# Mixture-of-experts stage of a decoder trunk: sixteen groups of 64 slots in plain fp32 in place of four groups of 128 slots in split fp32r

## What is computed

```python
def route_gates(xt, router_w, router_b):
    scores = jax.nn.sigmoid((xt @ router_w).astype(jnp.float32))
    sel = scores + router_b.astype(jnp.float32)
    # best of 4 groups by the sum of its two best experts, then its two best experts
    ...
    return jnp.sum(jax.nn.one_hot(idx, N_EXPERTS, dtype=jnp.float32) * w[..., None], axis=1)

def grouped_moe(x, router_w, router_b, w_gate, w_up, w_down):
    gates = route_gates(xt, router_w, router_b).astype(x.dtype)
    for e in range(N_EXPERTS):
        h = jax.nn.silu(xt @ w_gate[e]) * (xt @ w_up[e])
        out = out + gates[:, e:e + 1] * (h @ w_down[e])
```

## Time and profile before

| | |
|---|---|
| median of 3 runs | 905.53 us (905.52 to 907.23) |
| the profiled execution, its own time | 907.88 us |
| its span, first to last instruction | 906.1 us |
| PE matmuls busy | 88% of the span |
| DVE / ACT busy | 70% / 51% |
| loaded from memory | 174 MB, 193 GB/s over the span |
| mean granted clock of PE | 0.944 of 2.4 GHz |

### The profile page before, as it was taken

One profiled execution on the slowest core, in us unless ns is written; L12 is line 12 of the kernel. 1 busy time (PEld: TensorE's weight loads), 2 busy tenths in 40 slices (PEclk: granted clock), 3 DMA queues, 4 the chain that ended last, 5 costly groups with the idle time before them and its releaser, 6 DMA issues.

```text
span 906.1 us, 13457 instructions
## 1 busy us (share of the span) xinstructions
PE 794.1 (88%) x5124; PEld 715.8 (79%) x5124; DVE 634.4 (70%) x941; ACT 463.7 (51%) x684; POOL 46.2 (5%) x88
## 2 busy tenths in 40 slices
PE   4998899999957999999679889999998599999993
PEld 4987777888847898999469678777976499989992
DVE  4756864745485997889658487566355769979985
ACT  3445343455452776767333553344445347757761
POOL 3300000100050000000010000001000000000000
PEclk9999999999977999999969999999999599999997
DMA  9952035753254798799544221467423229968931
GB/s 288 348 184 94 24 116 188 230 187 140 81 188 142 293 360 323 258 350 311 180 139 141 94 93 47 146 206 253 146 87 140 93 97 383 350 239 324 345 121 48
DMA packets 62531, 176.15 MB, mean 194 GB/s; under 512 B 3856, under 2 KB 37056, under 8 KB 53248
## 3 DMA queue, kind: packets, MB, share of 16 engines
q1 hardware_dynamic: 57856, 162.80, 51.2%
q0 software_dynamic: 4032, 12.24, 4.4%
q10 hardware_dynamic: 576, 0.20, 0.1%
HBM read 174.18 MB, written 1.05 MB: 193 GB/s over the span
## 4 chain that ended last, share of the span: by engine, by line
PE 73%; DVE 14%; DVEq 4%; issue 4%; ACT 3%; DMA 1%; POOL 0%; ACTq 0%; POOLq 0%; SPq 0%
PE ring L1408 16%; PE ring L1410 15%; PE ring L1409 15%; PE quad L1408 5%; PE quad L1409 5%; PE quad L1410 5%; DVE w_lo L837 3%; PE ring L1672 2%; PE ring L1651 2%; PE quad L1766 2%; DVE x_lo L856 1%; ACT w_hi L560 1%; DMA raw<-in_w_in 1%; PE ring L1547 1%; PE ring L1721 1%
## 5 line engine op out<-in xcount | busy, mean ns | idle before, releaser
L837 DVE TENSOR_TENSOR w_lo<-raw,w_hi 128x1024 fp32r<-128x1024 f32 (+1 forms) x244 | 283.9, 1206 | 107.9 <-ACT w_hi L560 104.4
L560 ACT CAST w_hi<-raw 128x1024 fp32r<-128x1024 f32 (+1 forms) x244 | 240.4, 1038 | 114.4 <-PE quad L1410 83.7
L1408 PE MATMUL ring<-x_hi,w_hi 128*128 128x256 f32 x480 | 143.8, 300 | 19.7 <-DVE x_lo L856 9.1
L1409 PE MATMUL ring<-x_lo,w_hi 128*128 128x256 f32 x480 | 140.9, 293 | 0.0
L1410 PE MATMUL ring<-x_hi,w_lo 128*128 128x256 f32 x480 | 140.7, 293 | 0.0
L1408 PEld LDWEIGHTS ring<-x_hi,w_hi 128*128 128x128 f32 x480 | 97.4, 203 | 24.9 <-issue 11.0
L1409 PEld LDWEIGHTS ring<-x_lo,w_hi 128*128 128x128 f32 x480 | 97.4, 203 | 0.5 <-issue 0.5
L1410 PEld LDWEIGHTS ring<-x_hi,w_lo 128*128 128x128 f32 x480 | 97.3, 203 | 0.0
L1408 PE MATMUL ring<-w_hi,x_hi 128*128 128x256 f32 x288 | 82.6, 287 | 2.8 <-DVE x_lo L1292 2.8
L1410 PE MATMUL ring<-w_hi,x_lo 128*128 128x256 f32 x288 | 82.2, 285 | 0.0
L1409 PE MATMUL ring<-w_lo,x_hi 128*128 128x256 f32 x288 | 82.1, 285 | 0.0
(11 more groups left out here) (271 smaller groups left out, 1508.1 us busy)
## 6 DMA issues: line engine op xcount, KB each, us to landing
raw<-in_moe_w_gate SPq DMA_DIRECT2D x32, 1024.0 KB, 4.9
raw<-in_moe_w_up SPq DMA_DIRECT2D x32, 1024.0 KB, 5.0
raw<-in_moe_w_down SPq DMA_DIRECT2D x32, 1024.0 KB, 5.1
raw<-in_w_in SPq DMA_DIRECT2D x14, 1024.0 KB, 8.5
raw<-in_xattn_wk SPq DMA_DIRECT2D x8, 1024.0 KB, 6.9
raw<-in_w_out SPq DMA_DIRECT2D x8, 1024.0 KB, 5.0
raw<-in_xattn_wv SPq DMA_DIRECT2D x8, 1024.0 KB, 4.9
raw<-in_xattn_wq SPq DMA_DIRECT2D x8, 1024.0 KB, 5.7
```

The costliest lines, as they stand in the source:

```text
L560: nc.scalar.copy(unit_slot(u, 0, n)[:, s], raw[:, u % RAW_SLOTS, s]).then_inc(hi_done, 1)
L837: last = nc.vector.tensor_tensor(unit_slot(u, 1, n)[:, s], raw[:, u % RAW_SLOTS, s], unit_slot(u, 0, n)[:, s].bitcast(F32), ALU.subtract)
L1408: mm(out, a_hi, b_hi, start=first, stop=False)
L1409: mm(out, a_hi, b_lo, start=False, stop=False)
```

## The change

In the branch for tokens that fit, nothing of the expert weights is split any more. The raw ring has ten buffers for the experts (six raw ones, and the four places of `w_hi` and `w_lo`, seen as plain fp32), and PE multiplies straight from them in plain fp32. The order of loads is gate and up of a pair of experts, then the downs of the pair before.

Slots belong to an expert and no longer to a group of four: 64 slots each, 1,024 in all; the branch is taken if no expert has over 64 tokens. A token appears in the slots of both its experts. The gather runs in four quarters of 256 slots, and its result is only copied (half by ACT, half by DVE), no longer split. An even expert uses rows 0 to 63 of the PSUM banks, an odd one rows 64 to 127; a pair's hidden tiles are transposed together, copied by ACT, and its outputs, one expert in each half of the rows, are split and scattered with 8 matmuls for each pair. The general branch is written out without loops and reads the raw weights too.

```diff
+def expert_units(n):
+    order = []
+    for j in range(n // 2):
+        order += [(what, e) for e in (2 * j, 2 * j + 1) for what in "gu"]
+        if j:
+            order += [("d", 2 * j - 2), ("d", 2 * j - 1)]
+    return order + [("d", n - 2), ("d", n - 1)]
...
+    RING = RAW_SLOTS + 2 * SPLIT_SLOTS
+    SLOT = [u % RAW_SLOTS for u in range(U_MOE)]
+    SLOT += [m % RING for m in range(3 * E - 2)] + [RING - 2, RING - 1]
...
+        def of_pair(e):
+            return slice(EXPERT_SLOTS * (e % 2), EXPERT_SLOTS * (e % 2) + EXPERT_SLOTS)
...
-                for k in range(3):
-                    hi(U_MOE + k, l, NORMAL)
                 norm_stats(1, l)
...
-                lo(U_MOE + 1, l, NORMAL)
                 for t in range(T):
                     dve.wait_ge(xn_hi_done, l * T + t + 1)
...
-                for g in range(N_GROUPS):
+                for q in range(E // PER_GROUP):
                     for t in range(T):
-                        nc.vector.tensor_scalar(to_slot(t)[:, g * P:(g + 1) * P], slots[:], place[:, t, g:g + 1],
-                                                grv[:, t, g:g + 1], ALU.is_equal, ALU.mult)
...
+                        nc.vector.tensor_tensor(to_slot(t)[:, 256 * q:256 * q + 256].rearrange("p (e s) -> p e s", e=4),
+                                                view(slots[:], [[0, PER_GROUP], [1, EXPERT_SLOTS]]),
+                                                view(mine, [[1, PER_GROUP], [0, EXPERT_SLOTS]]), ALU.is_equal)
+                    dve.drain().then_inc(slots_ready, 1)
...
+                    def project_slots(e):
+                        if e >= 2:
+                            pe.wait_ge(h_ready, l * E + (e - 1))
+                            pe.wait_ge(turned_moved, l * PAIRS + e // 2)
+                        rows, q = of_pair(e), e // PER_GROUP
+                        s = slice(EXPERT_SLOTS * (e % PER_GROUP), EXPERT_SLOTS * (e % PER_GROUP) + EXPERT_SLOTS)
+                        for i, u in enumerate((gate_unit(e), up_unit(e))):
+                            pe.wait_ge(raw_full[SLOT[u]], landed(u, l))
+                            w = slot_view(u).rearrange("p (c n) -> p c n", c=DC)
+                            for c in range(DC):
+                                r = mm(ring[rows, i, 0:FF], slots_of(q)[:, c, s], w[:, c, :], start=c == 0,
+                                       stop=c == DC - 1)
+                            r.then_inc(unit_used, 1)
...
+                    def down(j):
+                        pe.wait_ge(turned_moved, l * PAIRS + (j + 1))
+                        if 0 < j < PAIRS - 1:
+                            pe.wait_ge(out_split, l * PAIRS + j)
+                        for e in (2 * j, 2 * j + 1):
+                            rows, u = of_pair(e), down_unit(e)
+                            pe.wait_ge(raw_full[SLOT[u]], landed(u, l))
+                            w = slot_view(u).rearrange("p (c n) -> p c n", c=2)
+                            for a in range(2):
+                                for c in range(2):
+                                    r = mm(out_bank(j, a)[rows, :], h_t[:, j % 2, c * P:(c + 1) * P][:, rows],
+                                           w[:, c, 512 * a:512 * a + 512], start=c == 0, stop=c == 1)
...
-                    for k in range(E):
...
+                    gather(0)
+                    pe.wait_ge(quad_free, l * (3 * T) + 2 * T)
+                    gather(1)
+                    gathered_rows(0)
...
+                    gates_of_slots()
+                    project_slots(0)
+                    gathered_rows(1)
+                    gather(2)
+                    project_slots(1)
+                    gathered_rows(2)
+                    to_token_turns()
+                    turn(0)
+                    project_slots(2)
+                    project_slots(3)
+                    pe.wait_ge(to_token_moved, l + 1)
+                    gather(3)
+                    turn(1)
+                    down(0)
+                    gathered_rows(3)
+                    for j in range(2, PAIRS):
+                        project_slots(2 * j)
+                        project_slots(2 * j + 1)
+                        scatter(j - 2)
+                        turn(j)
+                        down(j - 1)
+                    down(PAIRS - 1)
+                    scatter(PAIRS - 2)
+                    scatter(PAIRS - 1).then_inc(moe_done, 1)
```

More of the change, by code:

```diff
@@ L439, in _ @@
                     load(U_O + i, l, src, (2, D))
[L440 to L449, removed]
+                for m, (what, e) in enumerate(MOE):
+                    expert(l, e, what, U_MOE + m)
             for t in range(T):
@@ L762, in _ @@
                     act.sem_inc(act_emptied, 8)
[L764 to L772, removed]
@@ L788, in _ @@
                     last.then_inc(to_token_moved, 1)
[L789 to L798, removed]
@@ L1217, in _ @@
                 dve.wait_ge(act_emptied, emptied("rt1", l))
-                score, sel, rank, weight, grp = (rt[:, i] for i in range(1, 6))
+                score, sel, rank, weight, grp, member = (rt[:, i] for i in range(1, 7))
                 nc.vector.tensor_scalar(score, score, 1.0, None, ALU.add)
@@ L1339, in _ @@
-                    turned_low(E - 1)
-                    out_low(N_GROUPS - 1)
+                    nc.vector.tensor_scalar(slot_gates[:], ring[:, 3, 0:E], 0.5, None, ALU.mult)
+                    dve.drain()
+                    hidden(0)
+                    gather_move(2)
+                    hidden(1)
+                    for j in range(1, PAIRS):
+                        hidden(2 * j)
+                        hidden(2 * j + 1)
+                        if j == 1:
+                            gather_move(3)
+                        out_low(j - 1)
@@ L1735, in turn, with gates_of_slots @@
-                    def turn(k):
-                        pe.wait_ge(dve_emptied, l * DVE_LAYER + (DVE_AHEAD + 2 * (k + 1)))
+                    def gates_of_slots():
+                        for j in range(PAIRS):
+                            for t in range(T):
+                                r = mm(ring[:, 3, 2 * j:2 * j + 2], to_slot(t)[:, j * P:(j + 1) * P].bitcast(F32),
+                                       gates[:, t, 2 * j:2 * j + 2], start=t == 0, stop=t == T - 1)
+                        r.then_inc(slot_gated, 1)
@@ L1859, in _ @@
-                    step(2, 0, 0, first=True)
-                    step(3, 0, 0)
-                    with pe.Fori(1, STEPS) as i:
-                        step(2, i * 6, i * 2)
-                        step(3, i * 6, i * 2)
-                    moe_down(0, down_unit(E - 2), 0, E - 2)
-                    moe_down(1, down_unit(E - 1), 0, E - 1, last=True)
-                    pe.sem_inc(gathered, 8)
+                    for e in range(E):
+                        if e >= 2:
+                            pe.wait_ge(h_ready, l * E + (e - 1))
+                        moe_in(2 * (e % 2), gate_unit(e))
+                        moe_in(2 * (e % 2) + 1, up_unit(e))
+                        if e % 2 and e >= 3:
+                            moe_down(e - 3)
+                            moe_down(e - 2)
```

493 lines of the change are left out of this document (231 added, 262 removed).

## The result

The median of four runs is **941.2 us** (937.9 to 944.2) against 905.6 us before: ratio 1.0387, 95% interval 1.0350 to 1.0425. Slower, as forecast, by 35.5 us where the sum said 47.8. The profiled execution took 941.9 us, with a span of 940.1.

A forecast was written before the change was run, and what follows sets the result against it. TensorE was taken to set the pace; a stage of 182.7 + 7.3 = 190.0 us against 166.1 added 47.8 us over two layers, giving 953 us on the median's scale, with 920 to 980 us for 8 in 10.

The forecast's parts named there:

- The step on which it hung: Expert matmuls: halves meet for 3 matmuls of 32, so a 64-wide one costs 0.216 us like a 128-wide one.
- Gate, up and down: Expert stage, per layer: gate and up 110.6 less 5.2 us, down 55.0 less 10.3 and 7.0; together 143 us.
- Bank 0 behind ScalarE's copies: Expert 2's gate waits until ScalarE has copied four slot matrices and then the tile itself: 2.9 us with semaphores.
- The pair waits: Each later pair waits on its last hidden tile, mostly covered by a scatter: 0.3 x 7 = 2.0 us.
- Going between 64 and 128 wide: TensorE in the expert stage: each switch of matmul width waits 0.1 us, x 26 = 2.6 us.
- A fetch behind the written-out general branch: Jumping past the general branch may cost a code fetch: bounds 0 and 3 us a layer, taken as 0.
- Gather, slot gates and matrices, transposed tiles and scatter: Rest of TensorE's stage work, 39.6 us: gather 17.8, gates 3.4, slot matrices 1.7, hidden tiles 1.7, scatter 15.0.
- What would be seen: New profile: gate/up 0.216 us apart, downs 0.43, gapless PE, DVE and ScalarE below 30%, DMA near 300 GB/s, stage 190 us.
- rival 4: Clock falls while half of the array works; gate, up and down would double: above 1,200 us, chance 0.02.
- Rival 1: Array halves run fully beside each other and loads decide: stage 128 us, -38 a layer, 830 us; chance 0.11.
- Rival 2: Reach about twice as long, seven matmuls meet and not three: 21 us less a layer, 912 us; chance 0.08.
- Rival 3: Waits between pairs don't hide (hidden tile, transpose, ScalarE's copy, down): 1.5 us x 16 pairs, 977 us; chance 0.04.

The follow-up runs named there:

- call by call: Changed kernel with a pair's gate, up and down calls alternating between its two experts, one call each in turn, loads reordered to match: 842.5 us, ratio 0.9291.

## Why the prediction was right, point by point

**The step on which it hung** was that 64 wide costs as much as 128 wide unless the halves alternate within some 7 instructions. It held, with 4 matmuls and their loads in place of 3, and the experiments show it from both sides: the same arithmetic in another order takes 842.5 us. The rule quoted from the Trainium skill, "TensorE: Matmul & The Clock Gate", "The mechanism" of Part 3, that matmuls go strictly first in, first out, is contradicted by the windows around 348.93 us. The 2x of column tiling that the Trainium skill's "TensorEngine Tiling (Array Packing)", "When to Use Tiling", gives for 64 columns is real (64 matmuls in 6.91 us), but only in an order of issue that it does not ask for.

**Terms of the first layer's stage**, predicted 190.0 us, measured 185.9 (from the first gather to VectorE's start at 466.52 us):
- Gate, up and down: 143.1 predicted, 140.4 measured (9.37 + 7.05 + 14.88, six pairs of 16.70, 8.90). 4.0 of it is half clock that I had not seen coming (2.3 at expert 0, 1.7 at expert 2). Without it 136.4, so 6.7 us too much in the sum. The halves meet for 4 matmuls, not 3. For the downs, which also meet once more between the last two pairs, that is 9 x 4 x 0.43 = 15.5 us against 10.3. Gate and up meet seven times and not the eight of the sum, since a gather lies between experts 0 and 1: 7 x 4 x 0.216 = 6.0 against 5.2. The last three downs cover 1.4 us of the next gates in six pairs, 8.5 against 7.0. Together 7.5 us; some 0.8 of it goes back because the first matmul of a run takes longer (32 in 7.05 us, not 6.91).
- Waits: 7.3 predicted, 3.7 measured. Bank 0 behind ScalarE's copies: 2.9 predicted, 2.25 measured. The pair waits (2.0) did not come: in the steady pair each piece starts where the last ends, to 0.02 us. Going between 64 and 128 wide (2.6) costs no wait either, but it lengthens the pieces: behind 64-wide matmuls the scatter's 8 take 2.06 us where the kernel before's took 1.87, and the first of a gather 0.32 where the next take 0.12. Ten such places make 1.9 us, counted below. The type changes there too, from plain fp32 to fp32r in most of them, so what part is due to the width is not shown.
- A fetch behind the written-out general branch: bounds 0 to 3, I took 0. After the first layer's stage VectorE starts 1.42 us late with nothing in the profile to wait for, and 3.7 us late call by call (beyond my bound of 3), both times in the first layer only:
```profile
462.10 3.00 PE quad L1795 x12
465.10 1.42 issue
466.52 0.69 DVE X L942
```
- Gather, slot gates and matrices, transposed tiles and scatter: 39.6 predicted, 41.9 measured. The gates' 4.44 us for 3.4, the half clock again, is the largest part; the rest is the 0.2 us at each of the ten places, less 0.9 for the last four matmuls of the scatter, which VectorE doesn't wait for.

The errors are of both signs, and the sum came out 4.1 us too high in the first layer and 8.4 in the second. In the second (181.6 us) the gates take 3.47 us and expert 0 8.74, the first two gathers 9.15 for 10.45, and the 1.42 is missing. That the first layer came so close is in part luck: the half clock behind the gathers (5.0 us) and VectorE's late start (1.4), neither in the sum, made up for most of the 6.7 and of the waits that did not come. The mechanism was right; the term mis-sized most was the meetings of the halves.

**What would be seen**: single file at 0.216 and downs 0.43 apart, gate and up close to 13 us a pair (60 steps), PE without gaps in the pair, VectorE and ScalarE below 30%, loads near 300 GB/s at a share below 0.9: all there (331 GB/s and 0.86). The clock below 1.00 inside the stage, which I had named as a sign against, is also there, though behind the gathers it cost only 8.4 us in both layers together, and long stretches on half the array ran at 1.00, against rival 4.

**The rivals.** Rival 1 priced the halves fully beside each other at 830 us with the loads deciding. As built in this study it is 842.5: right in kind, with a rate of 418 GB/s and not 385, but with a hole in the loads between 310 and 320 us (139 GB/s) while PE does gathers, and 15 us of waiting at the end. Rival 2, twice the reach, is excluded by the 4 that meet. Rival 3 did not come: no wait ahead of a pair.

## What to carry to other kernels

Two 64-wide halves of the array doubled the rate of plain fp32 matmuls only where consecutive calls, or small blocks of up to four matmuls (two calls), alternate between them; a loop over experts that finishes one half before it begins the other leaves one idle, and each matmul costs the 0.216 us of a 128-wide one. Before such a change is judged, issue the same calls in alternating order, and only then ask what the deeper buffers are worth. Saving work on two engines that set no part of the stage (394 us of busy time here) did not make up for some 20 us a layer of added work on the one that does.

## What was not expected of the hardware

- At a hand-over 4 plain fp32 matmuls of each half overlap, whether they have 256 moving columns (0.216 us each) or 512 (0.43).
- The granted clock stood at half for 8 to 11 of the 256-column matmuls that follow PE's run of 2-column ones, without a gap between them, and again behind the wait of 2.25 us: 2.3 us once and 1.7 three times, 7.4 us in all, with 1.0 more inside the narrow run of the first layer. The wait alone is not enough: call by call, 64 matmuls behind the same 2.25 us take 7.13 us in the first layer, at full clock, and 8.79 in the second. What exactly lets the clock fall stays open.
- Loads of 1 MB ran at 415 to 421 GB/s in each 10 us from 330 to 390 us call by call, while PE read the ring's buffers at the doubled rate.
- VectorE started 1.4 to 3.8 us late behind the first layer's stage in all twelve profiles with the written-out general branch, 0.03 us or less behind the second, and at once in the kernel before. Two queues marked as instruction transfers moved 0.05 MB in 408 to 418 us call by call, but they move as much as 0.03 MB in 443 to 447 us of the kernel before as well. What makes VectorE late was not tried.
